# Splitting VectorE's gate step of the stick-breaking attention into three steps

## The chip, the cores and the metric

The kernel runs on one core of one Trainium2 chip. The metric is device time in microseconds (us) of that core, the median of several runs. One further run was recorded by the hardware profiler; all rows below are from that one.

## What is computed

Two transformer-like blocks on 512 tokens of width 1024. The part that matters here is the second layer of the first block, a stick-breaking attention with 16 heads of 64, followed by a gate and an output product:

```python
qz = h @ in_w                      # sb_in_w: q, then z
q, z = qz[..., :1024], qz[..., 1024:]
# per block of 128 queries: z_ = q k^T / 8, strictly causal mask
log_keep = where(mask, log_sigmoid(-z_), 0)
after    = reversed cumulative sum of log_keep, minus log_keep
a        = exp(log_sigmoid(z_) + after)
o        = a @ v
y        = (o * silu(z)) @ out_w   # sb_out_w
```

All dense products are done in float32 as three matmuls on split operands (high by high, high by low, low by high).

## The kernel before, in words

Every engine has its own instruction list, written as Python generators. A `yield` ends a step, and `weave((attention(), 111), (proj, 120))` merges two generators: the one with the smaller share of its length done goes next, attention first on a tie. TensorE, VectorE and ScalarE each have an `attention()` and a projection generator and use the same two lengths, so the merged orders agree from engine to engine. The engines meet only through semaphores, and each runs its own list in order.

**The attention.** There are 32 units, one for each of eight pairs of heads (n) and four blocks of 128 queries; unit a = 4n + i has (3 - i) + 1 blocks of 128 keys, so the widths of the units are 512, 384, 256, 128 and again. `attention()` runs rounds r = -1 to 35 of three steps each. What belongs to round r on each engine:

- TensorE: step 0, transposes of unit r-2 (L951, waits for `s_ls`, VectorE's product of that unit); step 1, weights times values of unit r-3 (L963); step 2, scores of unit r+1 (L975).
- ScalarE: step 0, the two sigmoids of unit r (L2309, L2310; the wait is for the scores and for VectorE's product of unit r-2); step 1, copy of the transposed unit r-2 (L2315); step 2, every fourth round, copy of the finished heads into QT (L2320, `s_o`).
- VectorE: step 0, two scans of unit r-1 (L1594, a running product instead of a sum of logarithms); step 1, one product of unit r-1 (L1600, signals `s_ls`).

**The projection `sb_proj()`.** After the columns of q (48 steps) come the columns of z, called `sz`: four groups i4 = 0 to 3 of 16 steps, with two blocks of 128 columns each. On TensorE a step is one k of a block, three matmuls (L658 to L660), so steps 1 to 8 are block 2 i4 and steps 9 to 16 are block 2 i4 + 1. On ScalarE step 1 splits off the high part of the next weight chunk (L1975), and step 16 has the two tanh (L2292, from the PSUM bank into T, `s_szt`) and, from i4 = 1, the high parts of the gated output (`so_high`, L2300, into SH). On VectorE step 9 makes the low part of the next weight chunk (`behind`, L1247, into wlo), and step 16 holds up to six operations:

- two gates: OZ = (tanh + 1) times the bank (L1575, wait for `s_szt`);
- from i4 = 1, two low parts of the heads of the group before: SL = OZ - SH (L1205, wait for ScalarE's SH);
- up to two `gate_att`: OZ = 0.5 times QT times OZ (L1560, wait for `s_o`).

Weight chunks are 1 MB, double buffered: a load (L487) waits until both parts of the chunk before it have been made.

Of the kernel before, what the change touches and what calls it, by code (L numbers as in the profile page):

```python
# [165 lines left out]
def idle(n):  # L166
    for _ in range(n):
        yield
# [30 lines left out]
def program(nc, wstream, astream, tstream, crow, vec, con, masks, xT, pT, rbx, out, scratch, pscr):  # L199
# [977 lines left out]
    def _(e):  # L1177
# [24 lines left out]
        def low(stage, k, src):  # L1202
            w.wait_ge(s_hh, HH_AT[stage, k])
            hi, lo = streams(stage)
            e.tensor_tensor(lo[:, k, :], src, hi[:, k, :].bitcast(F32), ALU.subtract).then_inc(s_hl["V"], 1)  # L1205
# [49 lines left out]
        def behind(kind, idx):  # L1255
            rest(chunk_of[kind, idx] + 1)
# [297 lines left out]
        def gate_att(n, src):  # L1554
            if n < 7:
                w.wait_ge(s_o, n + 1)
            else:
                w.wait_ge(s_av, 32)
            w.wait_ge(s_sz, n + 1)
            e.scalar_tensor_tensor(OZ[:, n, :], src, 0.5, OZ[:, n, :], ALU.mult, ALU.mult).then_inc(s_go, 1)  # L1560

        def sb_proj():
            yield
            yield
            for i4 in range(1, 4):
                yield from idle(8)
                behind("q", 2 * i4)
                yield from idle(8)
            for i4 in range(4):
                yield from idle(8)  # L1570
                behind("sz", 2 * i4)
                yield from idle(7)
                for n in (2 * i4, 2 * i4 + 1):
                    w.wait_ge(s_szt, n + 1)
                    e.scalar_tensor_tensor(OZ[:, n, :], T[n % 3][:, :], 1.0, bank_of("sz", n)[:, :],  # L1575
                                           ALU.add, ALU.mult).then_inc(s_sz, 1)
                if i4 > 0:
                    for n in (2 * i4 - 2, 2 * i4 - 1):
                        low("so", n, OZ[:, n, :])
                for n in (2 * i4, 2 * i4 + 1):  # L1580
                    if n < 7:
                        gate_att(n, QT[:, n, :])
                yield

        def attention():

            own(e.memset(keeps[:, :, S:S + 1], 0.0))
            for r in range(-1, 36):
# [13 lines left out]
                yield  # L1602

        proj = sb_proj()
        next(proj)
        next(proj)
# [1112 lines left out]
```

## Time and profile before

| | |
|---|---|
| median of 3 runs | 1558.29 us (1556.65 to 1560.05) |
| profiled run, its own time | 1557.7 us |
| its span | 1555.8 us |
| TensorE busy | 1540.1 us (99%) |
| VectorE busy | 950.0 us (61%) |
| ScalarE busy | 678.1 us (44%) |
| GpSimd busy | 97.4 us (6%) |

An engine's busy time counts its instructions' durations, overlaps counted once; the rest of the span it waited or sat between instructions. The engine that is busy nearly all of the span sets the time; a wait on another counts only if it reaches that one. In a timeline row the bracket gives the idle time ahead of the instruction and whose work ended it. Consecutive alike instructions stand in one row with their count. TensorE's matmuls overlap: a row's duration is longer than the distance to the next one.

### The profile page before, as it was taken

To read this page: it belongs to the slowest core of one execution; us is meant where nothing else is said; L and a number is where in the kernel's file an instruction comes from. 1 tells how busy PE (TensorE), PEld (TensorE's weight loads), DVE (VectorE), ACT (ScalarE), POOL (GpSimd) and SP (SyncE) were. 2 spreads that over 40 slices of the span, in tenths; PEclk is the share of its full clock that TensorE was granted. 3 is DMA by queue.
4 is the path that set the end of the run, shared out by engine and by line. 5 is a ranking of instruction groups with operands and counts; after the bars stand their busy time and mean duration, and the time that the engine had idled before them with its cause. 6 is when DMAs were issued, how large, how long until landed. Compare 5 with 4: busy or idle time off the path is not lost. (4 is left out here: it accounts for less than half of the span.)

```text
span 1555.8 us, 19263 instructions
## 1 busy us (share of the span) xinstructions
PE 1540.1 (99%) x7806; PEld 1219.5 (78%) x7806; DVE 950.0 (61%) x1211; ACT 678.1 (44%) x958; POOL 97.4 (6%) x66
## 2 busy tenths in 40 slices
PE   8999999999999999999999999999999999999998
PEld 4788887778788666678898886678888888888887
DVE  4769898996874666755468446754553434432445
ACT  4556567754532655654222455533442222322232
POOL 0000001011300000023000000000120000000110
PEclk8999999999999999999999999999999999999999
DMA  9245334433793111123211122222223222222233
GB/s 389 103 149 176 135 123 135 149 108 139 260 357 108 56 55 46 37 82 111 82 55 55 55 82 95 68 82 89 101 82 108 86 104 99 91 102 102 78 112 122
DMA packets 47383, 177.72 MB, mean 114 GB/s; under 512 B 3616, under 2 KB 20512, under 8 KB 31680
## 3 DMA queue, kind: packets, MB, share of 16 engines
q1 hardware_dynamic: 30368, 167.44, 29.8%
q10 hardware_dynamic: 16928, 9.06, 2.2%
q8 instruction: 62, 1.02, 0.3%
q14 instruction: 25, 0.20, 0.0%
HBM read 172.23 MB, written 4.26 MB: 113 GB/s over the span
## 5 line engine op out<-in xcount | busy, mean ns | idle before, releaser
L658 PE MATMUL bank<-HH,whi 128*128 128x512 f32 x1352 | 556.0, 411 | 0.4 <-issue 0.4
L660 PE MATMUL bank<-HH,wlo 128*128 128x512 f32 x1352 | 528.7, 391 | 0.0
L659 PE MATMUL bank<-HL,whi 128*128 128x512 f32 x1352 | 527.8, 390 | 0.0
L1247 DVE TENSOR_TENSOR wlo<-raw,whi 128x2048 fp32r<-128x2048 f32 (+2 forms) x122 | 267.2, 2190 | 105.8 <-ACT whi L1975 105.0
L658 PEld LDWEIGHTS bank<-HH,whi 128*128 128x128 f32 x1352 | 254.3, 188 | 80.9 <-issue 33.8
L660 PEld LDWEIGHTS bank<-HH,wlo 128*128 128x128 f32 x1352 | 254.1, 188 | 54.8
L659 PEld LDWEIGHTS bank<-HL,whi 128*128 128x128 f32 x1352 | 254.8, 188 | 47.9 <-issue 3.8
L1975 ACT ACTIVATE whi<-raw 128x2048 fp32r<-128x2048 f32 (+2 forms) x118 | 222.5, 1885 | 126.0 <-PE bank L660 108.3
L2577 POOL TENSOR_TENSOR SR<-SR,tmp 128x512 f32<-128x512 f32 x35 | 62.0, 1772 | 596.0 <-ACT tmp L1995 595.0
L1594 DVE TENSOR_TENSOR_SCAN W<-W,cc 128x511 f32<-128x511 f32 (+3 forms) x64 | 49.0, 808 | 34.6 <-ACT W L2310 34.5
L660 PE MATMUL bank<-FH,wlo 128*128 128x512 f32 x176 | 68.5, 389 | 0.0
L658 PE MATMUL bank<-FH,whi 128*128 128x512 f32 x176 | 68.5, 389 | 0.0
L659 PE MATMUL bank<-FL,whi 128*128 128x512 f32 x176 | 68.5, 389 | 0.0
L1906 DVE TENSOR_TENSOR pst<-bank,SR 128x512 f32<-128x512 f32 x22 | 15.1, 692 | 72.0 <-PE bank L660 72.0
L1918 DVE SCALAR_TENSOR_TENSOR tmp<-tmp,bank 128x512 f32<-128x512 f32 x22 | 15.1, 688 | 65.0 <-PE bank L660 65.0
L2546 ACT ACTIVATE FH<-tmp 128x512 fp32r<-128x512 f32 x22 | 13.9, 632 | 85.9 <-DVE tmp L1918 85.9
L2542 ACT ACTIVATE tmp<-pst 128x512 f32<-128x512 f32 x22 | 13.9, 632 | 82.4 <-DVE pst L1906 82.4
L1995 ACT ACTIVATE tmp<-X 128x512 f32<-128x512 f32 x35 | 21.6, 626 | 61.5 <-DVE X L1466 44.8
L2577 POOL TENSOR_TENSOR SR<-SR 128x512 f32<-128x512 f32 x12 | 20.0, 1665 | 338.8 <-ACT SR L1995 338.8
L2137 ACT ACTIVATE E<-AC,atk 128x128 f32<-128x128 f32 x128 | 39.1, 392 | 4.5 <-DMA AC<-scratch 4.5
L2309 ACT ACTIVATE W<-zz 128x1024 f32<-128x1024 f32 (+3 forms) x32 | 22.6, 707 | 41.1 <-PE zz L975 37.3
L658 PE MATMUL bank<-WH,whi 128*128 128x512 f32 x96 | 38.9, 405 | 0.0
(326 smaller groups left out, 2225.6 us busy)
## 6 DMA issues: line engine op xcount, KB each, us to landing
raw<-wstream SPq DMA_DIRECT2D x113, 1024.0 KB, 4.9
aslot<-tstream SPq DMA_DIRECT2D x24, 512.0 KB, 3.6
A<-astream SPq DMA_DIRECT2D x8, 1024.0 KB, 20.4
AC<-scratch ACTq DMA_DIRECT2D x16, 512.0 KB, 5.2
QT<-tstream SPq DMA_DIRECT2D x12, 512.0 KB, 6.9
OZ<-tstream SPq DMA_DIRECT2D x12, 512.0 KB, 8.7
raw<-wstream SPq DMA_DIRECT2D x4, 768.0 KB, 4.9
X<-xT SPq DMA_DIRECT2D x1, 2048.0 KB, 8.3
```

What stands on the lines that cost most here:

```text
L658: e.matmul(o, wh[:, k, c], hi[:, kb0 + k, :], start=first and k == 0, stop=False)
L659: e.matmul(o, wh[:, k, c], lo[:, kb0 + k, :], start=False, stop=False)
L660: x = e.matmul(o, wl[:, k, c], hi[:, kb0 + k, :], start=False, stop=last and k == kb - 1)
L1247: x = e.tensor_tensor(wlo[:, i % 2, c], raw[:, i % 2, c], whi[:, i % 2, c].bitcast(F32), ALU.subtract)
L1594: x = e.tensor_tensor_scan(k, k, diag[:, last], 0.0, ALU.mult, ALU.add)
L1906: e.tensor_tensor(pstage[n % 3][:, :], bank_of("fg", n)[:, :], R, ALU.mult).then_inc(s_fgr, 1)
L1918: e.scalar_tensor_tensor(q, q, 0.5, bank_of("fu", n)[:, :], ALU.mult, ALU.mult).then_inc(s_fu, 1)
L1975: e.activation(whi[:, i % 2, 0:n], raw[:, i % 2, 0:n], ACT.Copy).then_inc(s_hi, 1)
L1995: e.activation(dst, src, ACT.Square, scale=scale).then_inc(s_sq, 1)
L2137: x = e.activation(E[(u + 1) % 2][:, h, :], AC[:, h, :], ACT.Relu, scale=-1.0, bias=atk[:, cv_, 8 * gv + h:8 * gv + h + 1])
L2309: e.activation(keep(a, S - hi, S), zz[:, :, 0:hi], ACT.Sigmoid, scale=-1.0)
L2577: e.tensor_tensor(acc, acc, tile, ALU.add).then_inc(s_sqa, 1)
```

## The change

Inside each of the four groups of `sz` on VectorE, the low part of the weight chunk is made two steps earlier (after 6 idle steps, not 8), and the block of up to six operations of step 16 becomes three steps: the two gates in step 14, the two low parts in step 15, the two `gate_att` in step 16. The group still has 16 steps. No operation is added or removed, and the other engines' lists stay as they were.

```diff
             for i4 in range(4):
-                yield from idle(8)
+                yield from idle(6)
                 behind("sz", 2 * i4)
                 yield from idle(7)
                 for n in (2 * i4, 2 * i4 + 1):
                     w.wait_ge(s_szt, n + 1)
                     e.scalar_tensor_tensor(OZ[:, n, :], T[n % 3][:, :], 1.0, bank_of("sz", n)[:, :],
                                            ALU.add, ALU.mult).then_inc(s_sz, 1)
+                yield
                 if i4 > 0:
                     for n in (2 * i4 - 2, 2 * i4 - 1):
                         low("so", n, OZ[:, n, :])
+                yield
                 for n in (2 * i4, 2 * i4 + 1):
                     if n < 7:
                         gate_att(n, QT[:, n, :])
                 yield
```

## Rows read from the trace of the kernel before

**Rows 1.** The page: busy time by engine, and the granted clock over 40 slices.

```profile
PE 1540.1 (99%) x7806; PEld 1219.5 (78%) x7806; DVE 950.0 (61%) x1211; ACT 678.1 (44%) x958; POOL 97.4 (6%) x66
...
PEclk8999999999999999999999999999999999999999
```

**Rows 2.** Waits of TensorE, whole span: us in total, times, longest.

```profile
PE zz L727 <- DVE SR L1259: 1.5, 1, 1.5
...
PE tt L951 <- DVE W L1600: 0.9, 2, 0.7
```

**Rows 3.** Waits of TensorE from 690 us to the end, first and last of three.

```profile
PE tt L1085 <- DVE tmp L1819: 0.4, 1, 0.4
...
PE tt L1085 <- DVE PS L1819: 0.2, 1, 0.2
```

**Rows 4.** Waits of VectorE between 540 and 720 us.

```profile
DVE OZ L1575 <- ACT tmp L2292: 20.0, 8, 5.9
```

**Rows 5.** Timeline around the gates of group 0: start, us, engine, line, operation.

```profile
600.10 1.80 DVE L1594 TENSOR_TENSOR_SCAN W<-W,cc 128x383 f32<-128x383 f32 x2 [0.56 <-ACT W L2310]
...
601.93 0.96 DVE L1600 TENSOR_TENSOR W<-W 128x768 f32<-128x768 f32 x1
...
605.77 0.69 DVE L1575 SCALAR_TENSOR_TENSOR OZ<-tmp,bank 128x512 f32<-128x512 f32 x1 [2.88 <-ACT tmp L2292]
...
606.82 0.69 DVE L1575 SCALAR_TENSOR_TENSOR OZ<-tmp,bank 128x512 f32<-128x512 f32 x1 [0.36 <-ACT tmp L2292]
...
607.31 0.81 PE L951 MATMUL tt<-cc,W 128*128 128x128 f32 x6
607.43 1.29 DVE L1560 SCALAR_TENSOR_TENSOR OZ<-QT,OZ 128x512 f32<-128x512 f32 x2
```

**Rows 6.** Timeline around the low part of the weights in group 1.

```profile
614.52 2.34 DVE L1594 TENSOR_TENSOR_SCAN W<-W,cc 128x511 f32<-128x511 f32 x2 [2.79 <-ACT W L2310]
...
616.77 2.27 DVE L1247 TENSOR_TENSOR wlo<-raw,whi 128x2048 fp32r<-128x2048 f32 x1
```

**Rows 7.** Timeline around the gates of group 1.

```profile
622.80 1.26 DVE L1594 TENSOR_TENSOR_SCAN W<-W,cc 128x255 f32<-128x255 f32 x2
...
624.09 0.69 DVE L1600 TENSOR_TENSOR W<-W 128x512 f32<-128x512 f32 x1
...
629.98 0.69 DVE L1575 SCALAR_TENSOR_TENSOR OZ<-tmp,bank 128x512 f32<-128x512 f32 x1 [1.23 <-ACT tmp L2292]
...
630.59 1.29 DVE L1205 TENSOR_TENSOR SL<-OZ,SH 128x512 fp32r<-128x512 f32 x2
...
631.79 1.29 DVE L1560 SCALAR_TENSOR_TENSOR OZ<-QT,OZ 128x512 f32<-128x512 f32 x2
631.80 0.60 PE L951 MATMUL tt<-cc,W 128*128 128x128 f32 x4
...
632.70 1.01 ACT L2309 ACTIVATE W<-zz 128x1024 f32<-128x1024 f32 x1
...
634.73 0.92 PE L975 MATMUL zz<-KT,QT 64*128 64x384 f32 x4
```

**Rows 8.** Timeline around the gates of group 2.

```profile
644.84 0.73 DVE L1594 TENSOR_TENSOR_SCAN W<-W,cc 128x127 f32<-128x127 f32 x2
...
651.45 0.69 DVE L1575 SCALAR_TENSOR_TENSOR OZ<-tmp,bank 128x512 f32<-128x512 f32 x1 [5.89 <-ACT tmp L2292]
...
654.14 1.29 DVE L1560 SCALAR_TENSOR_TENSOR OZ<-QT,OZ 128x512 f32<-128x512 f32 x2
...
655.34 0.42 DVE L1600 TENSOR_TENSOR W<-W 128x256 f32<-128x256 f32 x1
...
655.82 0.44 PE L951 MATMUL tt<-cc,W 128*128 128x128 f32 x2 [0.72 <-DVE W L1600]
```

**Rows 9.** Stretches of the start: length, busy us by engine, PEclk, DMA share, GB/s.

```profile
14.00:15.00 1.00, 0.00 (x0) 0.00 (x0) 0.90 (x2) 0.77 (x2) 0.00 (x0) 1.00 0.95 389
...
20.00:40.00 20.00, 18.67 (x126) 11.44 (x118) 11.48 (x19) 7.68 (x13) 0.00 (x0) 0.75 0.98 408
```

## The prediction

> **What bounds the kernel now.** I began with the busy times and the clock: TensorE is busy 1540.1 of 1555.8 us, at full clock in all slices but the first [rows 1]. So the question is only whether TensorE waits more or less than before. Its list of waits comes next: the longest single one is 1.5 us, at the start, and in the attention only its transposes (L951) wait for VectorE's product (L1600), 0.9 us in two places [rows 2]. After 690 us it waits three times, between 0.2 and 0.4 us, 0.9 us in all [rows 3]. What the change can give is therefore about 0.9 us in its own stage, and any delay made there finds almost no slack further on that could take it up. The third view is VectorE's waits: all eight gates (L1575) waited for ScalarE's tanh, 20.0 us together, the longest 5.9 us [rows 4]. That is the wait which the change moves. The last view is the timeline around groups 0, 1 and 2, for what stands behind it.
>
> **Where the gates go in VectorE's list.** Projection step p runs once more than (p-1)/120 of the 111 attention steps are done; 48 steps belong to q, and three attention steps are a round, beginning with -1. In group 0 the gates were step p = 64, which needs 59 attention steps: 18 rounds and 5 steps, so rounds up to 17 and steps 0 and 1 of round 18. They now are p = 62, which needs 57: rounds up to 17 only. The scans and the product of unit 17 (round 18) stood ahead of the gates and now stand behind them, with the product also behind step 15. In the same way, in group 1 (gates p = 80 to 78, needing 74 and now 72) the scans of unit 22 go behind the gates and its product behind gates and low parts. In group 2 (p = 96 to 94, needing 88 and now 87) the gates and low parts were already ahead of unit 27's product but behind its scans; now the scans are behind them too. In group 3 (p = 112 to 110) steps 103 and 101 separate them, which is step 2 of round 32 and step 0 of round 33: both empty on VectorE, as unit 31 was the last. Nothing moves there.
>
> ScalarE's tanh stay in step 16, and the second of them needs TensorE's last matmul of step 16. So VectorE's wait ends when it did, but it begins earlier in the list, and what it used to do before the wait it does after it. TensorE needs that work soon: transposes of unit 17 are step 0 of round 19, two short steps (scores of unit 19, one k of the next block) after the matmul on which the gates wait.
>
> **The cost, group by group.** All starts are from the profiled run.
>
> Group 0: the second gate starts at 606.82 as before, since nothing of TensorE or ScalarE ahead of it changes. The next VectorE instruction then started 0.61 us later, at 607.43 [rows 5]; that now is the scans of unit 17, 1.80 us, to 609.23. There are no low parts in group 0. The product follows 0.03 us behind the scans as in its row (600.10 + 1.80 to 601.93) and takes 0.96 us: end 610.22. From end to TensorE's start was 0.06 us in the one place where it waited (655.34 + 0.42 = 655.76 to 655.82 [rows 8]): the transposes start at 610.28, not at 607.31. **+2.97 us.** Next late is `gate_att` of heads 0 and 1 (1.29 us) and unit 18's scans (1.26 us) and product; they end near 613.5. From unit 17's transposes to unit 22's TensorE took 24.5 us [rows 5, 7], 4.9 us a unit, so it wants unit 18 near 615. Nothing is added.
>
> Group 1: the second gate starts at 629.98. Scans of unit 22 start at 630.59 and take 1.26 us, to 631.85; the two low parts, whose SH is ready by then, take a further 1.20 us to the next start (630.59 to 631.79), so the product starts at about 632.99 and takes 0.69: end 633.68, transposes at 633.74, not 631.80 [rows 7]. **+1.94 us.** ScalarE's sigmoids of unit 24 wait for the same product; the first of two alike started at 632.70 and took 1.01 us. Started at 633.7 they end by 635.8, ahead of the scores that need them (634.73 + 1.94 = 636.67 [rows 7]). So it is one delay, counted once.
>
> Group 2: here TensorE already waited 0.72 us for unit 27's product [rows 8]. Its scans (0.73 us, 0.08 of it under the next instruction's start) now come between the low parts and `gate_att`. The product starts 0.65 us later. **+0.65 us.**
>
> Group 3: 0, by the count above.
>
> The low part of the weights (2.27 us) moves two steps ahead, past one unit's scans in groups 1, 2 and 3, and in group 0 past unit 15's. I cost it at nothing. In group 1 it ran after unit 20's scans, ahead of which VectorE had been idle for 2.79 us [rows 6]: it now fills that idle time, and unit 20's product can end about 2 us earlier, for which nobody waits, as that product is not among TensorE's waits [rows 2]. If that cover were gone, it would still cost nothing: the low part stood between the scans and the product before, so what lies ahead of the product stays the same. It also lets SP issue the next weight load about 2 us earlier; it has a whole group (some 20 us) to land in, and no matmul of this stage waits for weights.
>
> The sum: 2.97 + 1.94 + 0.65 = 5.56 us. Against the profiled run's own 1557.7 (span 1555.8 and 1.9 around it) that is 1563.3. That run is 0.6 below the median, 1558.3, with which the changed kernel will be compared, so I take 1558.3 + 5.6 = **1563.9 us**, 0.36% slower.
>
> For the bounds: the order of the three stalls is counted, only their sizes are open. The least is the scans alone after the gates (1.80 + 0.73 and no product, if that found some slack that I do not see), about 3.2 us with group 1's 0.7; the most is the sum with each moved piece whole, without the overlaps of 0.08 us and with a further late unit in each group, about 7 us.
>
> One bound is the clock. At the start, TensorE had whole microseconds with nothing to do (14 to 15), and from 20 to 40 us its granted clock was 0.75 in the mean with the engine busy for 18.67 us: half of that time at 1.2 GHz, half at 2.4 [rows 9]. The stall in group 0 leaves TensorE idle for about 2.8 us, from 607.5 to 610.3. If the clock fell there, matmuls start at twice the distance for as long as there, 10 us, or, as the work here is denser, perhaps 4, which costs half of it, 2 to 5 us. Later the clock never shows a fall [rows 1], but no gap was as long, so the trace can't decide it. The start had several gaps in a row and very small matmuls between; here dense work stands on both sides, which is why I leave it out of the sum.
>
> The Trainium skill, page "TensorE: Matmul & The Clock Gate", section "Why this matters for your kernels", warns that idle gaps between bursts of matmuls put the clock back to its lower level, which speaks against a change that makes them; by it the sum could be that of the clock rival below. By that rule, the trace agrees: the clock is down after the start's gaps.
>
> **The rivals.**
>
> *The clock falls in group 0's stall* (also possible in group 1's, where it is shorter). For: rows 9. Against: one gap only, dense around. Time 1563.9 + 2 to 5 = 1566 to 1569.
>
> *The split works as spacing and TensorE waits less.* If the gates found the tanh ready at step 14, unit 27's product would stand 1.3 us sooner relative to its neighbours and the 0.9 us of waits would go: 1558.3 - 0.9 = 1557.4, no measurable change. It decides if the tanh of a group ends before VectorE reaches step 14. Against: the gates waited in all eight cases even at step 16, 2.5 us on average [rows 4], and the tanh's input is not finished before TensorE's step 16. For a gain over 0.2% (3.1 us) there is no room at all in this stage's waits.
>
> *The delay is taken up.* VectorE runs one to two rounds ahead of TensorE, and each product has slack (unit 22's ended at 624.78, 7 us before use [rows 7]). If the stalls shrink to half, the time is 1561.1, and under 1561.4 is within what I call no change. Against: the slack is measured from where the product stood before the wait; after it the arithmetic above leaves none.
>
> **How the numbers follow.** Forecast as summed 0.79, clock 0.10, taken up by half or more 0.07, spacing works 0.04. About 0.2%, 3.1 us, is what a measurement of this kernel can tell. Faster by more: 0.01, out of the spacing case. No change: 0.10, from the last two. Slower: 0.89. The forecast's own bounds are +3.2 to +7, 1561.5 to 1565.3; towards the clock case the range is taken up to 1567, and below to 1561.
>
> **What the profile of the changed kernel would show.** Gates in the same places relative to the last matmul of their block; directly behind them in groups 0, 1, 2 the scans of 383, 255 and 127 columns; TensorE's transposes waiting on L1600 (now a few lines lower in the file) about 2.8, 1.8 and 1.4 us, total some 6 us where it was 0.9; VectorE idle longer ahead of the first gate in groups 0 and 1 by the scans and product moved (about 2.8 and 2.0 us), and the granted clock 1.00 between 600 and 680. I am wrong if the transposes of units 17 and 22 start unwaited, if the clock shows 0.50 there, or if a later wait of TensorE shrinks by as much.

## The result: 0.46% slower, by three waits and a fall of the clock

| | before | changed |
|---|---|---|
| median | 1557.55 us (10 runs) | 1565.91 us (10 runs) |
| ratio to before, 95% interval | | 1.0046 (1.0037 to 1.0055) |
| profiled run's span | 1555.8 us | 1563.1 us |

The median lies inside the range of 1561 to 1567, 2 us above the forecast of 1563.9. The 0.46% of the ratio are 7.2 us of the median before, against 5.6 forecast; the two profiled spans differ by 7.3 us. The two medians lie further apart, 8.4 us: of the ten times before, five are at most 1556.8 and five at least 1558.3, and their median stands in the gap between. One run of e6 below took 1697.45 us, 9% above all others of its kernel; it is a slow one and in no ratio.

The first view of the profile after is TensorE's list of waits over the whole span, as in [rows 2]: who waits for whom, us in total, times, longest. L1602 is the product that was L1600.

```profile
PE tt L951 <- DVE W L1602: 6.0, 4, 2.8
PE zz L727 <- DVE SR L1259: 1.5, 1, 1.5
...
PE tt L1085 <- DVE tmp L1821: 0.4, 1, 0.4
...
PE tt L1085 <- DVE PS L1821: 0.2, 1, 0.2
```

What was 0.9 us in two places is 6.0 us in four. The late waits [rows 3] are what they were. From unit 27's transposes to the end of the span it is 900.0 us before (655.82 to 1555.8) and 900.1 now (662.99 to 1563.1), so nothing was given back. VectorE's waits between 540 and 720 us, as in [rows 4]:

```profile
DVE OZ L1575 <- ACT tmp L2294: 27.8, 8, 7.1
```

The gates wait 7.8 us more, and still all eight wait: VectorE idles 3.35 us longer ahead of the first gate of group 0 (2.88 to 6.23), 3.32 in group 1 (3.28 to 6.60) and 1.26 in group 2 (5.89 to 7.15). The timeline around group 0, which answers to [rows 5]:

```profile
606.07 0.69 DVE L1575 SCALAR_TENSOR_TENSOR OZ<-tmp,bank 128x512 f32<-128x512 f32 x1 [6.23 <-ACT tmp L2294]
...
607.12 0.69 DVE L1575 SCALAR_TENSOR_TENSOR OZ<-tmp,bank 128x512 f32<-128x512 f32 x1 [0.36 <-ACT tmp L2294]
...
607.72 1.80 DVE L1596 TENSOR_TENSOR_SCAN W<-W,cc 128x383 f32<-128x383 f32 x2
609.55 0.96 DVE L1602 TENSOR_TENSOR W<-W 128x768 f32<-128x768 f32 x1
610.43 1.28 DVE L1560 SCALAR_TENSOR_TENSOR OZ<-QT,OZ 128x512 f32<-128x512 f32 x2
610.57 1.54 PE L951 MATMUL tt<-cc,W 128*128 128x128 f32 x6 [2.80 <-DVE W L1602]
...
611.76 0.78 PE L658 MATMUL bank<-HH,whi 128*128 128x512 f32 x1
...
615.95 1.13 PE L975 MATMUL zz<-KT,QT 64*128 64x512 f32 x4
```

The reader is to see two things. The scans of 383 columns and the product stand behind the second gate, and TensorE's transposes start 3.45 us after that gate's start; before it was 0.49 (606.82 to 607.31). That is +2.96. And the six transposes take 1.54 us instead of 0.81, the next matmul 0.78 instead of 0.48. The clock explains that: in e6, e9 and e10 below, where the six also start after a wait but at full clock, they take 0.87 to 0.88. Stretches of the changed kernel, with the same columns as [rows 9] (the granted clock is the third number from the end):

```profile
20.00:40.00 20.00, 18.66 (x129) 11.46 (x121) 11.36 (x19) 7.69 (x13) 0.00 (x0) 0.76 0.98 407
600.00:620.00 20.00, 17.20 (x104) 11.18 (x103) 11.29 (x15) 10.02 (x15) 0.00 (x0) 0.91 0.10 32
...
609.00:610.00 1.00, 0.00 (x0) 0.00 (x0) 0.96 (x2) 0.37 (x1) 0.00 (x0) 1.00 0.00 0
610.00:613.00 3.00, 2.43 (x9) 2.01 (x9) 2.96 (x6) 1.47 (x3) 0.00 (x0) 0.50 0.00 0
```

The same 20 us before:

```profile
600.00:620.00 20.00, 20.00 (x128) 12.91 (x126) 13.77 (x17) 11.29 (x18) 0.00 (x0) 1.00 0.00 1
```

0.91 over 20 us is some 3.6 us at 1.2 GHz; shorter stretches of the same trace give 3.4, from 610.0 to 613.4. So the clock fell 0.6 us before the transposes started, with TensorE idle since 607.8. What it cost can be read between two fixed points of TensorE's list, from unit 17's transposes to the scores of unit 20: 5.38 us (610.57 to 615.95), where the same work took 4.06 before (607.31 to 611.37): +1.32 us. Less than 0.1 us of that is the start after a wait and not the clock: e5, e6 and e9 show 4.13 to 4.15 at full clock.

Group 1, which answers to [rows 7], and group 2, which answers to [rows 8]:

```profile
634.56 0.69 DVE L1575 SCALAR_TENSOR_TENSOR OZ<-tmp,bank 128x512 f32<-128x512 f32 x1 [1.23 <-ACT tmp L2294]
...
635.17 1.26 DVE L1596 TENSOR_TENSOR_SCAN W<-W,cc 128x255 f32<-128x255 f32 x2
...
636.35 1.27 DVE L1205 TENSOR_TENSOR SL<-OZ,SH 128x512 fp32r<-128x512 f32 x2
637.53 0.68 DVE L1602 TENSOR_TENSOR W<-W 128x512 f32<-128x512 f32 x1
...
638.27 0.66 PE L951 MATMUL tt<-cc,W 128*128 128x128 f32 x4 [1.73 <-DVE W L1602]
...
658.00 0.69 DVE L1575 SCALAR_TENSOR_TENSOR OZ<-tmp,bank 128x512 f32<-128x512 f32 x1 [7.15 <-ACT tmp L2294]
...
660.68 0.73 DVE L1596 TENSOR_TENSOR_SCAN W<-W,cc 128x127 f32<-128x127 f32 x2
661.33 1.27 DVE L1560 SCALAR_TENSOR_TENSOR OZ<-QT,OZ 128x512 f32<-128x512 f32 x2
662.51 0.42 DVE L1602 TENSOR_TENSOR W<-W 128x256 f32<-128x256 f32 x1
...
662.99 0.44 PE L951 MATMUL tt<-cc,W 128*128 128x128 f32 x2 [1.34 <-DVE W L1602]
```

From gate to transposes group 1 took 1.82 us before (629.98 to 631.80) and now 3.71: +1.89. In group 2, from the first gate, 4.37 (651.45 to 655.82) became 4.99: +0.62. The gates of group 0 already stood 0.30 us later (606.82 to 607.12), ahead of the first wait that changed; e3 shows that the earlier low part of the weights, the only moved work ahead of them, delays nothing, so this is taken as a difference between two executions. With it the sum is 0.30 + 2.96 + 1.32 + 1.89 + 0.62 = 7.09 of the 7.3 us, and 6.79 of it belong to the change.

### The profile page after: what moved, and what is told of

Same layout as the page of the kernel before. It is cut to its first block and busy times, and to the rows that moved or that the text cites. A ratio compares the mean times of both kernels' runs of the same rounds, so it can differ in the third digit from the quotient of the medians.

```text
span 1563.1 us, 19263 instructions
## 1 busy us (share of the span) xinstructions
PE 1541.7 (99%) x7806; PEld 1220.2 (78%) x7806; DVE 949.7 (61%) x1211; ACT 678.6 (43%) x958; POOL 97.7 (6%) x66
```

## The experiments

Two theories stood against each other in size: the waits alone (5.6 us), or the waits and the clock that the longest of them lets fall (7 us). A third was that the other parts of the edit cost too. In the table, "clock" is the granted clock in the stretch around group 0 of the profiled run, and the last column is the distance between the two fixed points above, where it was read.

| run | ratio to before (95%) | TensorE waits for L951's input, 600 to 690 us | clock 600 to 620 | transposes 17 to scores 20 |
|---|---|---|---|---|
| before | 1 | 0.7 | 1.00 | 4.06 |
| changed | 1.0046 (1.0037 to 1.0055) | 2.8 + 1.7 + 1.3 | 0.91 | 5.38 |
| e1, group 0 alone | 1.0031 (1.0019 to 1.0042) | 2.8 + 0.7 | 0.91 | 5.69 |
| e2, groups 1 and 2 | 1.0014 (1.0005 to 1.0023) | 1.7 + 1.4 | 1.00 | |
| e3, weights early | 1.0002 (0.9993 to 1.0011) | 0.7 | 1.00 | |
| e4, changed again | 1.0043 (1.0031 to 1.0056) | 6.0 whole span | 0.83 | 6.78 |
| e5, filled | 1.0037 (1.0025 to 1.005) | 3.5 whole span | 1.00 | 4.15 |
| e6, gates in step 15 | 1.001 (1.0 to 1.0019) | 1.0 + 1.3 | 1.00 | |
| e7, split after | 1.0002 (0.9993 to 1.001) | 0.3 | 1.00 | |
| e8, tanh early | 1.0003 (0.9994 to 1.0012) | none | 1.00 | |
| e9, group 0 filled | 1.0021 (1.0012 to 1.0031) | 0.3 + 0.7 | 1.00 | 4.13 |
| e10, gates in step 13 | 1.0039 (1.0026 to 1.0053) | 5.9 | 0.91 | 5.65 |

**e1 and e2: the groups apart.** The edit of the changed kernel, made for some groups only:

```diff
-                yield from idle(8)
+                early = i4 in (0,)            # e2: (1, 2)
+                yield from idle(6 if early else 8)
...
+                if early:
+                    yield
                 if i4 > 0:
                     ...
+                if early:
+                    yield
```

> Only group 0 has the new steps (weights two steps earlier, gates in step 14, the rest in steps 15 and 16). If the wait at the head of VectorE's list is the cause and nothing else: one TensorE wait of about 2.8 us for unit 17's product and 3.0 us more time; with the short fall of the clock seen in the changed kernel's profile (1.3 us) 4.3 us more. No wait for unit 22's product; unit 27's as before, 0.7 us. Rival, that the stages after the gates or the weights cost time too: more than 4.5 us.

> Only groups 1 and 2 have the new steps. By the wait: TensorE waits 1.7 and 1.3 us for the products of units 22 and 27, 1.9 + 0.6 = 2.5 us more time than before, granted clock 1.00 throughout since no stall is as long as group 0's. If shorter stalls let the clock fall as well: 3 to 5 us more and a stretch below 1.00. If the parts do not add: e1 and e2 together differ from the changed kernel's 7 to 8 us by more than 1.5 us.

e1: 1.0031 is 4.8 us; e2: 1.0014 is 2.2 us. Together 7.0, the changed kernel's 7.2. e1 has unit 17's wait of 2.8 us and the slow stretch; e2 has its two waits and no slow stretch, so 1.7 us of idling did not lower the clock. One thing was expected otherwise: 4.3 us for e1, and more than 4.5 if other parts cost too. The 4.8 lie above that line, but their interval, 1.0019 to 1.0042, is 3.0 to 6.5 us and holds both, so the timing does not decide it; the rows do. TensorE in e1:

```profile
610.13 1.46 PE L951 MATMUL tt<-cc,W 128*128 128x128 f32 x6 [2.80 <-DVE W L1605]
611.24 0.78 PE L658 MATMUL bank<-HH,whi 128*128 128x512 f32 x1
...
615.82 1.13 PE L975 MATMUL zz<-KT,QT 64*128 64x512 f32 x4
```

The wait costs 3.0 us as counted; the stretch behind it, mostly by the slow clock, adds 5.69 - 4.06 = 1.6: together 4.6 of the 4.8.

**e3: the low part of the weights alone.**

```diff
-                yield from idle(8)
+                yield from idle(6)
                 behind("sz", 2 * i4)
-                yield from idle(7)
+                yield from idle(9)
```

> Only the low part of the weights is made two steps earlier in all four groups; gates, low parts and gate_att stay together in step 16. By my prediction: no change, within 0.1%, TensorE's waits as before (0.9 us for VectorE's products). Rival, that the earlier weight load or the moved scans cost something: up to 2.3 us more.

Ratio 1.0002, waits as before. That part of the edit costs nothing that can be measured. The low parts and `gate_att` by themselves were not tried in their new steps; but since the rows above already add up to 7.09 of 7.3 us, little is left for them or for the third theory.

**e4: the changed kernel again.**

> The changed kernel once more, for the same chip as e1 to e3 and a second look at the clock after the stall of group 0. By the sum of stalls and the clock 7 us more than before; if the clock falls only by the chance of its phase, this profile may show it at 1.00 there and a span of 1.3 us less, or a longer low stretch.

The ratio, 1.0043, is 6.7 us, for 7 expected. The profile shows the same 2.80 us wait and with it a longer slow stretch: 0.83 over the 20 us is 6.8 us at 1.2 GHz, and 6.78 us between the fixed points, +2.72.

```profile
610.98 1.54 PE L951 MATMUL tt<-cc,W 128*128 128x128 f32 x6 [2.80 <-DVE W L1602]
...
600.00:620.00 20.00, 17.20 (x92) 11.45 (x90) 10.64 (x15) 9.06 (x15) 0.00 (x0) 0.83 0.08 20
```

So the clock's part changes from run to run, 1.3 to 2.7 us, while the waits stay. Part of that goes with where the slow stretch begins. In the changed kernel and e4 the clock fell 0.6 and 1.0 us before the transposes started, in e1 and e10 0.1 and 0.9 us behind their start. Of the 3.4 us of slow clock the changed kernel thus spent 0.6 idling and lost 1.3 us, while e1 and e10 worked through all of it and lost 1.6.

**e5 and e9: the stall filled with work.** TensorE's list gets 11 matmuls, on data that lie in SBUF, ahead of unit 17's transposes. Their product is not used: the transposes overwrite it.

```diff
                 for a in live(r - 2):
+                    if a == 17:
+                        w.wait_ge(s_at, a)
+                        for _ in range(11):
+                            e.matmul(tt[:, 0, :], HL[:, 0, 0:128], HH[:, 0, :], start=True, stop=True)
                     w.wait_ge(s_ls, a + 1)
```

> The changed kernel, with 11 matmuls of 512 columns added on TensorE right ahead of unit 17's transposes; their product lands in tt, which the transposes overwrite. They fill about 2.5 us of the 2.8 us stall of group 0 with work. If the idle time lets the clock fall: granted clock 1.00 between 600 and 620, the mean clock of all runs back at before's (0.9964), and 5.6 us more than before instead of 7. If the clock is lowered for another reason, or costs nothing: 7 us more, as the changed kernel.

> Only group 0 changed, as e1, and the 11 matmuls of e5 ahead of unit 17's transposes. By the wait in order plus the clock: the clock stays at 1.00 there, 3.0 us more than before where e1 had 4 to 5, mean clock as before's. If the clock was no part of e1's time: the same 4 to 5 us more.

TensorE in e9, where L948 is the filling:

```profile
608.57 0.40 PE L660 MATMUL bank<-HH,wlo 128*128 128x512 f32 x1
608.80 2.67 PE L948 MATMUL tt<-HH,HL 128*128 128x512 f32 x11
611.76 0.87 PE L955 MATMUL tt<-cc,W 128*128 128x128 f32 x6 [0.29 <-DVE W L1609]
...
615.89 0.70 PE L979 MATMUL zz<-KT,QT 64*128 64x512 f32 x2
...
600.00:620.00 20.00, 19.71 (x120) 13.35 (x121) 10.18 (x15) 11.18 (x16) 0.00 (x0) 1.00 0.00 1
```

The transposes still start 2.96 us later than they could (608.80 to 611.76), since VectorE is no faster. But the clock stays at 1.00, and the distance to the scores is 4.13, nearly the 4.06 of before (the row above ends its window inside the scores, so it counts two of the four). The same in e5: 4.15. The fall is thus a consequence of TensorE's idling, shown by filling it, in two profiles against four with the stall unfilled. The mean granted clock of all runs, which e5's expectation names, says nearly the same: 0.9960 in e5 and 0.9963 in e9, where before has 0.9964; unfilled it is 0.9948 in the changed kernel, 0.9946 in e4 and 0.9940 in e1. e10 is the exception, 0.9960 with a fall in its profile; the clock of the start moves this mean too. In time e9 has 3.3 us (1.0021) where e1 has 4.8; e5 has 5.8 where the changed kernel has 7.2. The steps have the expected size, but the intervals overlap, so it is the clock rows that decide, not the timings.

**e6 and e10: one step later, one step earlier.** In e6 the gates are in step 15 in all groups, and low parts and `gate_att` in step 16:

```diff
-                yield from idle(8)
+                yield from idle(6)
                 behind("sz", 2 * i4)
-                yield from idle(7)
+                yield from idle(8)
                 for n in (2 * i4, 2 * i4 + 1):
                     ...
+                yield
                 if i4 > 0:
```

In e10 the gates are in step 13 in groups 0 to 2:

```diff
-                yield from idle(8)
+                yield from idle(6)
                 behind("sz", 2 * i4)
-                yield from idle(7)
+                yield from idle(6 if i4 < 3 else 7)
                 for n in (2 * i4, 2 * i4 + 1):
                     ...
+                yield
+                if i4 < 3:
+                    yield
                 if i4 > 0:
                     ...
+                yield
```

> All groups: weights two steps early, the two gates in step 15 (one step early, not two), low parts and gate_att in step 16. By the count the scans of unit 17 then stand ahead of the gates of group 0, its product behind; in group 1 the product of unit 22 comes directly behind the gates; group 2 as in the changed kernel. From the rows: +1.15 us in group 0, 0 in group 1, +0.65 in group 2, in all +1.8 us, clock as before. If any early gate costs as the changed kernel's: +5 us and more.

> Gates one step earlier still in groups 0 to 2 (step 13), group 3 as in the changed kernel. Between step 13 and 14 VectorE's merged list holds no attention work in these groups, so the same instructions stand behind the gates: TensorE's waits as in the changed kernel (2.8, 1.7, 1.3 us), time 7 us above before. If the cost goes by the number of steps and not by what is passed: half as much again, 10 us.

e6 has 1.6 us (1.001), for 1.8 expected; e10 has 6.1 (1.0039), for 7. Neither fits a price per step, which would have them at half and at one and a half of the changed kernel, 3.6 and 10.8 us: their intervals end at 3.0 and 8.3. The rows say it more sharply, since e6 has no wait in group 1 at all and e10 has the changed kernel's waits. e6's group 0, where only the product is behind the gates:

```profile
605.32 0.69 DVE L1575 SCALAR_TENSOR_TENSOR OZ<-tmp,bank 128x512 f32<-128x512 f32 x1 [0.36 <-ACT tmp L2293]
...
605.92 0.95 DVE L1601 TENSOR_TENSOR W<-W 128x768 f32<-128x768 f32 x1
...
606.93 0.87 PE L951 MATMUL tt<-cc,W 128*128 128x128 f32 x6 [0.96 <-DVE W L1601]
```

From gate to transposes 1.61 us, 1.12 more than the 0.49 of before; 1.15 was expected.

**e7 and e8: splits that hold nothing up.** e7 keeps the gates in step 16 and puts the low parts and `gate_att` one and two steps behind, for groups 0 to 2:

```diff
-                yield from idle(8)
+                yield from idle(6 if i4 else 8)
...
+                if i4 < 3:
+                    yield
                 if i4 > 0:
                     for n in (2 * i4 - 2, 2 * i4 - 1):
                         low("so", n, OZ[:, n, :])
+                if i4 < 3:
+                    yield
```

e8 leaves VectorE an operation in step 14, but one whose tanh is there by then:

```diff
 # ScalarE
-                yield from idle(15)
+                yield from idle(9)
                 for n in (2 * i4, 2 * i4 + 1):
...
+                    if n % 2 == 0:
+                        yield from idle(6)
 # VectorE, idle(6) before the weights, idle(7) behind
                 for n in (2 * i4, 2 * i4 + 1):
...
+                    if n % 2 == 0:
+                        gate_att(n, QT[:, n, :])
+                        yield
+                        yield
...
+                if i4 < 3:
+                    gate_att(2 * i4 + 1, QT[:, 2 * i4 + 1, :])
```

> Split the other way: in groups 0 to 2 the gates stay in step 16, the low parts follow one step later and gate_att two steps later, at the start of the next group, so that scans and products of the attention come between them. If VectorE's queue behind the gates is what TensorE feels: the wait for unit 27's product (0.7 us) vanishes, time 0.7 us less than before, which the timing hardly tells (ratio 0.999 to 1.000). If the split itself costs: a new wait.

> ScalarE makes the tanh of a group's first block in step 10 instead of 16; VectorE does that block's gate and gate_att in step 14 and the second gate, the low parts and the other gate_att in step 16; weights two steps early. The early gate finds its tanh ready, so it holds nothing up: no wait for unit 17 or 22, unit 27's about 0.1 us instead of 0.7, time 0 to 0.7 us less than before. If an operation of VectorE in step 14 costs by itself, wait or not: 1 us and more above before.

Both took away TensorE's wait for unit 27, e7 wholly (the 0.3 us left are at the transposes of unit 28), e8 too. Group 2 in e7:

```profile
654.16 0.69 DVE L1575 SCALAR_TENSOR_TENSOR OZ<-tmp,bank 128x512 f32<-128x512 f32 x1 [0.19 <-ACT tmp L2296]
654.77 0.42 DVE L1604 TENSOR_TENSOR W<-W 128x256 f32<-128x256 f32 x1
...
655.10 1.29 DVE L1205 TENSOR_TENSOR SL<-OZ,SH 128x512 fp32r<-128x512 f32 x2
...
656.77 0.38 PE L951 MATMUL tt<-cc,W 128*128 128x128 f32 x2
```

The product comes directly behind the gates and is done at 655.19, 1.6 us before TensorE starts on it. The times, 1.0002 and 1.0003, cannot tell 0.7 us from nothing; neither is shown to be faster than the kernel before. What e8 does show is that an early operation is harmless if nothing in it waits: its four early gates start without a wait, and no wait of TensorE for L951's input is left between 600 and 690 us.

## Why the prediction was right

- **The order of the work.** Right in all groups: scans and product of unit 17, scans and product of unit 22, scans of unit 27 behind the gates, nothing in group 3. e1 shows group 0 by itself, e2 groups 1 and 2 without it.
- **The terms.** Group 0: 2.97 forecast, 2.96 measured. Group 1: 1.94 and 1.89. Group 2: 0.65 and 0.62. TensorE's waits were forecast as 2.8, 1.8 and 1.4 us and read as 2.80, 1.73 and 1.34. One step inside group 1 does not add up: scans that start at 630.59 and take 1.26, and 1.20 for the low parts, put the product at 633.05, not 632.99, and the term at 2.00. The 1.94 needs an overlap that the text does not name there; the rows after have it (635.17 + 1.26 to 636.35, 0.08 us).
- **The low part of the weights.** Costed at nothing; e3 measured 1.0002.
- **VectorE's idle time.** Forecast 2.8 and 2.0 us longer ahead of the first gates of groups 0 and 1, measured 3.35 and 3.32. In group 0 the 0.56 us that stood idle ahead of unit 17's scans joined it. In group 1 the low part of the weights no longer stood ahead of unit 20's product, so unit 21's product was done 1.4 us earlier against the gates (621.92 to 629.98 before, 625.09 to 634.56 after), and that time too went to the wait. It cost TensorE nothing.
- **What was too small.** The clock was left out of the sum and given a chance of 0.10. It fell after group 0's stall in all four profiles that have it unfilled (changed, e1, e4, e10) and in neither that has it filled; it cost 1.3 to 2.7 us there. My grounds for leaving it out, one gap only with dense work on both sides, did not hold. By the prediction's own signs it was wrong here: it expected 1.00 between 600 and 680 us and called a clock of 0.50 there a sign of being wrong, and the rows show 0.50 from 610.0 to 613.4. The price in the rival, 2 to 5 us, reaches from the upper half of what was measured to above it; its lower end stood on a slow stretch of 4 us that no row of before shows, and measured were 3.4 and 6.8. The term of the sum that was wrong is this one: 0 instead of 1.3 to 2.7 us, which brings 5.6 to between 6.9 and 8.3, with the 7.2 of the ratio inside.
- **The bounds.** The upper one, 7 us for the waits, was not needed for the waits; the three waits cost 5.5 us. The median, 1565.9, lies above the forecast's own bound of 1565.3; the range held it because it had been drawn towards the clock case, to 1567. So the three waits were foreseen, and that the range held is owed to a case given 0.10.
- **The rivals.** Spacing that helps did not come with the gates in step 14, but it does exist in the other direction: e7 takes away the wait, though no time could be measured. Nothing took the delay up: the late waits stayed, and so did the time from group 2 to the end.

Not tried: the gates in step 13 in group 3 too. By the same count unit 31's product would stand behind gates whose tanh needs TensorE's step 16, and that step stands behind unit 31's transposes. The engines would wait for each other in a circle; one step separates the changed kernel from that.

## What to carry to other kernels

To cost a moved operation, ask first whether it waits, and for what. If what it waits for comes at a fixed point of another engine's list, moving it forward doesn't move it in time; it moves everything that it passes to behind that point. The price is the length of what was passed, less the slack to its reader, and it is paid once for each place: e6, the changed kernel and e10 differ by one step each and cost 1.6, 7.2 and 6.1 us, since only the work passed counts. If TensorE is the bound engine and idles for 2.8 us, as here, look also at its clock in the rows after.

## What the runs showed of the hardware

- A stall of 2.8 us of TensorE, in the middle of dense work (granted clock 1.00 from 40 to 600 us), brought in all four profiles a stretch at 1.2 GHz, 3.4 us long in three of them and 6.8 in e4. It began between 1.0 us before the end of the stall (e4) and 0.9 us behind it (e10), so the first matmuls behind a stall can still run at full clock. Stalls of 1.7 us brought none (e2, and group 1 of the changed kernel, e4, e5 and e10). Eleven matmuls in the gap kept the clock at 1.00 (e5, e9).
- The Trainium skill, page "TensorE: Matmul & The Clock Gate", section "Why this matters for your kernels", warns of idle gaps between bursts of matmuls. These rows agree, and they show it for a gap of 2.8 us.
- The spread of the kernel before, 1555.9 to 1561.0 us, goes with its clock. In the profiles the clock is below 1.00 only in the first 40 us, apart from the stretch behind the stall; for runs without a profile, that it is the start is not shown. Of the 64 runs of it that stand beside e1 to e10, the 24 with a mean granted clock of 0.995 have a mean span of 1557.8 us, the 20 with 0.998 or 0.999 one of 1554.3. In the profiles the stretch from 20 to 40 us has 0.75 before, 0.91 in e2 and 1.00 in e10, where no edit touches it:

```profile
20.00:40.00 20.00, 17.07 (x151) 11.01 (x152) 12.16 (x24) 8.87 (x15) 0.00 (x0) 1.00 0.98 405
```

That is e10. The spread by this, 3.5 us, is larger than what the longest stall costs here without the clock, 2.96, and five to eleven runs of a kernel hardly see through it.
